# Issuing the gates' last tile in portions between the experts' fetches, in both product-key expert layers

## What is computed

```
act = gelu(einsum('pkd,pd->pk', expert_u[ib], tb)) * gate
out = einsum('pk,pkd->pd', act, expert_v[ib])
```

## Time and profile before

| | |
|---|---|
| median of 3 runs | 4310.23 us (4307.28 to 4312.26) |
| the profiled execution: its own time, its span | 4309.91 us, 4308.1 us |
| PE busy | 3590.4 us, 83% of the span |
| DVE, ACT busy | 2167.2 us (50%), 1557.5 us (36%) |
| wide layer: last tile's store issued, experts' loop ends | 1130 us, about 2065 us |
| narrow layer: the same | 2509.7 us, about 3010 us |
| mean granted clock of TensorE | 0.908 |

### The profile page before, as it was taken

The page is one execution under the profiler, slowest core; times in us unless marked ns, Lnnn a source line. Parts: engine busy times, 40 slices in busy tenths (PEclk is TensorE's granted clock), DMA queues, the critical chain, the costliest instruction groups (busy, mean ns, idle before and its releaser), DMA issues. The chain is left out here.

```text
span 4308.1 us, 55843 instructions
## 1 busy us (share of the span) xinstructions
PE 3590.4 (83%) x19731; PEld 2623.5 (61%) x19731; DVE 2167.2 (50%) x4184; ACT 1557.5 (36%) x2599; POOL 182.2 (4%) x358
## 2 busy tenths in 40 slices
PE   7967978968799999999798479999887867777766
PEld 5747966437688888888567469999656322222222
DVE  4534643799766666666445978888442000000001
ACT  4433442218644434444241466666221111101111
POOL 0006610000000000000000000000100000000000
PEclk8888989989999999999899789999878888888888
DMA  5220021523645545555402089997304799999997
GB/s 189 104 93 13 14 102 45 191 87 157 252 165 193 170 170 195 166 175 195 145 1 88 30 331 335 312 311 240 132 31 174 325 428 427 428 428 428 427 428 320
DMA packets 300729, 909.70 MB, mean 211 GB/s; under 512 B 46736, under 2 KB 150928, under 8 KB 273552
## 3 DMA queue, kind: packets, MB, share of 16 engines
q1 hardware_dynamic: 300560, 907.42, 55.7%
HBM read 854.38 MB, written 52.95 MB: 211 GB/s over the span
## 5 line engine op out<-in xcount | busy, mean ns | idle before, releaser
L1995 PE MATMUL po<-act_parts,v_parts 128*128 128x512 f32 x2048 | 482.0, 393 | 10.7 <-DVE v_parts L2075 4.2
L1982 PE MATMUL pd<-h_parts,u_parts 128*128 128x512 f32 x2048 | 474.2, 392 | 17.5 <-DVE u_parts L2070 17.5
L1982 PEld LDWEIGHTS pd<-h_parts,u_parts 128*128 128x128 f32 x2048 | 387.3, 189 | 99.3 <-DVE u_parts L2070 18.2
L1995 PEld LDWEIGHTS po<-act_parts,v_parts 128*128 128x128 f32 x2048 | 382.7, 188 | 105.1 <-DVE v_parts L2075 22.5
L3543 PE MATMUL pb<-moe_ring_more,moe_xs 128*32 128x512 f32 x2048 | 326.3, 740 | 127.5 <-DMA moe_ring_more<-in_moe_gu 125.9
L3625 DVE TENSOR_TENSOR moe_hidden<-moe_silu,pg 128x512 f32<-128x512 f32 x16 | 11.0, 688 | 575.1 <-PE pg L3532 533.1
L2214 PEld LDWEIGHTS pd<-h_parts,u_parts 128*128 128x128 f32 x2048 | 264.8, 192 | 18.4 <-DVE u_parts L2295 7.4
L2224 PE MATMUL po<-v_parts,act_parts 128*128 128x512 f32 x1024 | 261.5, 400 | 16.6 <-DVE act_parts L2311 16.6
L2214 PE MATMUL pd<-h_parts,u_parts 128*128 128x256 f32 x2048 | 267.9, 284 | 6.8 <-DVE u_parts L2295 6.8
L3568 PE MATMUL pd<-moe_ring_more,moe_hidden 128*32 128x512 f32 x1024 | 167.8, 791 | 107.5 <-DMA moe_ring_more<-in_moe_down 99.3
L395 PE MATMUL ps<-h_terms,w_terms 128*128 128x512 f32 x960 | 225.9, 399 | 36.2 <-DVE w_terms L408 36.2
(11 more groups left out here) (505 smaller groups left out, 5789.1 us busy)
## 6 DMA issues: line engine op xcount, KB each, us to landing
moe_ring_more<-in_moe_gu SPq DMA_DIRECT2D x128, 2048.0 KB, 36.1
u_stream<-in_peer_u SPq DMA_DIRECT2D x256, 512.0 KB, 6.3
v_stream<-in_peer_v SPq DMA_DIRECT2D x256, 512.0 KB, 4.9
moe_ring_more<-in_moe_down SPq DMA_DIRECT2D x64, 2048.0 KB, 36.9
ada_ring<-in_ada_w SPq DMA_DIRECT2D x20, 2048.0 KB, 14.0
g_stream<-peer_gates SPq DMA_DIRECT2D x128, 256.0 KB, 6.1
w_stream<-in_gdn_w_in SPq DMA_DIRECT2D x8, 2048.0 KB, 8.1
w_stream<-in_peer_wq SPq DMA_DIRECT2D x8, 2048.0 KB, 9.2
```

The lines of the kernel that those rows point to most:

```text
L1982: m = pe.matmul(pd[:, j, 0:T], us[:, j, w, c], h[:, w, c], start=(c + w == 0), stop=(c == DC - 1 and w == 1))
L1995: m = pe.matmul(po[:, (c + b) % 4, 0:T], vs[:, j, w, (c + b) * P:(c + b) * P + P], aparts[:, 4 * half + j, w], start=(j + w == 0), stop=(j ...
```

## The change

Four edits in the listing. First, `LastTile` keeps `gates` and the stage, and `write` takes the portions to issue. The scatter now issues portions 0 and 1 in the wide layer, only portion 0 in the narrow one. Second, the wide layer's SP issues portions 2 and 3 after u of period 1. Third, in the wide layer ACT and DVE do all four `high_u(1)` and `low_u(1)` ahead of the first `gate`; ACT does squash 0 and 1 between them and squash 2 and 3 after its wait for portions 1 to 3. Fourth, the narrow layer's SP issues portion 1 after two pairs of gates and v, portion 2 after four pairs, and portion 3 after u 4 to 7, right ahead of the wait for it. No arithmetic is added or taken away, and no byte.

```diff
@@ peer_scatter, SP
-                last.write(sp, gates, stage[(tiles - 1) % 2])
+                last.write(sp, *((0, 1) if T == TALL else (0,)))
@@ LastTile
-    def __init__(self, k, tiles):
+    def __init__(self, k, tiles, gates, stage):
         self.tile = tiles - 1
+        self.gates, self.stage = gates, stage
...
-    def write(self, eng, gates, stage):
-        for n in range(self.PARTS):
+    def write(self, eng, *parts):
+        for n in parts:
             rows = slice(n * self.ROWS, (n + 1) * self.ROWS)
-            eng.dma_start(gates[self.tile, :, rows], stage[:, rows]).then_inc(self.landed[n].h, DMA_DONE)
+            eng.dma_start(self.gates[self.tile, :, rows], self.stage[:, rows]).then_inc(self.landed[n].h, DMA_DONE)
@@ experts_wide, SP
                 for j in range(4):
                     get_u(1, j, False)
+                last.write(sp, 2, 3)
                 last.wait(sp, 0)
                 for j in range(4):
                     get_g(0, j, True)
@@ experts_wide, ACT
                 for j in range(4):
-                    squash(0, j, True)
+                    if j < 2:
+                        squash(0, j, True)
                     high_u(1, j)
-                    if j == 0:
-                        last.wait(sc, 1, 2, 3)
+                last.wait(sc, 1, 2, 3)
+                for j in range(4):
+                    if j >= 2:
+                        squash(0, j, True)
                     high_a(0, 0, j, True)
@@ experts_wide, DVE
                 for j in range(4):
+                    low_u(1, j)
+                for j in range(4):
                     gate(0, j)
-                    low_u(1, j)
                     low_a(0, 0, j)
@@ experts_narrow, SP
                 for j in range(HALF):
                     get_g(0, j)
                     get_v(0, j)
+                    if j == 1:
+                        last.write(sp, 1)
+                last.write(sp, 2)
                 for j in range(HALF, RAW):
                     get_g(0, j)
                 last.wait(sp, 1, 2)
                 for j in range(HALF, RAW):
                     get_u(0, j)
+                last.write(sp, 3)
                 last.wait(sp, 3)
                 for j in range(HALF, RAW):
                     get_v(0, j)
```

More of the change, by code:

```diff
@@ L2371, in peer_layer @@
         gain = k.sb(ctx, "peer_gain", [DC, 2])
-        last = LastTile(k, T // P)
         tables = k.sb(ctx, "u_stream", [4, DC, P])
@@ L2376, in peer_layer @@
             odd = k.sb(place, "gate_stage_odd", [P, P])
+        last = LastTile(k, T // P, gates, (even, odd)[(T // P - 1) % 2])
         u, v = W[f"peer_u{layer}"], W[f"peer_v{layer}"]
```

## The result

The changed kernel takes 4317.92 us (median of 18 runs, 4309.09 to 4327.42) against 4311.57 us before (18 runs, 4307.28 to 4316.85). The ratio is 1.0016, with a 95% interval of 1.0009 to 1.0022: some 7 us slower. I had said 4309.8 with a range to 4315.5; 1.3 us of the distance is that the kernel before itself now stands at 4311.57, where its first three runs had given 4310.23. The loss is smaller than the 0.2% that I had named as the limit, but with the runs made it is clear of the noise, and it went the way that I gave to a rival.

What follows compares the result with a forecast made beforehand. PE alone bounds both loops, so the change acts only at the two starts. From 4309.91, wide -2.3 and narrow +2.0 gave 4309.6 profiled, 4309.9 on the median; stated 4309.8, range 4301 to 4315.5.

Steps and rivals of the forecast that it cites:

- The path: Both starts: first(1) at 1155.3, job 2 waits 3.7 us; narrow second(0) 11.7 us earlier, second(4) held by v 4.
- the narrow layer's queue times: Narrow start: from 2521.6, gates and v pairs 3.4 us, portions 4.9, u 4 to 7 1.25 each; v 4 lands 2556.0.
- The second(4) that I put 2.0 us late: Narrow start: waiting for v 4, second(4) starts at 2558.9 instead of 2556.91; 2.0 us lost, bounds 0 and 6.
- rival B: Narrow start: queue-full stalls delay portion 2 or 3, v 4 lands at 2561.7, 7.7 us lost, total 4315.3; chance 0.17.
- the clock at first(4): Narrow start: first(4) comes 1.3 us earlier, but at half clock after ten idle us, which eats that gain.
- The wide term: Wide start: `low_v` 3 ends at 1180.9 instead of 1183.2, 2.3 us gained; range kept 0.7 to 2.3.
- no loss: Wide start: new waits, shorter than 8.80 us, cost nothing in clock; if it falls, 1.64 of the 2.3 us is lost.
- Rival C: Wide start does nothing, u no earlier or clock falls: 0 to 0.7 gained, 2.0 lost, 4311.5; chance 0.15.
- The price of one DMA: Narrow start: v table into an empty queue 3.5 us by the trace, 3.2 by the skill's fit (loss then 1.6).

Runs made afterwards that it cites:

- n1: Narrow layer's edits alone (wide layer as before), with portion 3 issued together with portion 2, ahead of gates 4 to 7; run once, 4323.08 us.
- t1: Wide layer as before; narrow scatter issues portions 0 to 2, only portion 3 goes out behind u 4 to 7; run once, 4315.14 us.
- t4: Narrow layer's edits alone, plus 96 added matmuls ahead of first(4), overwritten; run once, 4319.85 us.
- e2: The narrow-only kernel: the change's narrow edits, wide layer as before; 4318.97 us, ratio 1.0016 (1.0007 to 1.0025) against before.
- e1: The wide-only kernel: the change's wide edits, narrow layer as before; 4311.64 us, ratio 0.9998 (0.9989 to 1.0007) against before.
- e3: Wide layer's portions moved as in the change, but ACT and DVE in the order of before; narrow layer as before; run once, 4316.38 us.
- ww: Wide edits plus v 0 and v 1 fetched and split ahead of the gates, narrow layer as before; 4311.52 us, ratio 0.9997 (0.9988 to 1.0006).
- e4: Wide layer's edits alone, plus 16, 5 and 8 added matmuls in PE's three waits, overwritten; 4312.78 us, ratio 0.9998 (0.9989 to 1.0007).

## Why the prediction was wrong

**The path was right, in both layers.** The gates land at the same distance as before (35.55 from the first fetch, before 35.53); first(1) starts at 28.6 without a wait (forecast 1155.3 less 1126.66, also 28.6); job 2 waits 3.79 us for squash 2 (3.7); the splits of v 2 and v 3 hold second(0). In the narrow layer second(0) moves 11.6 us forward (11.7), first(4) waits for u 4, and second(4) waits for v 4, which stands behind portion 3. The two halves and n1, t1 and t4 moved these landings, and the starts followed.

**The step that failed is the narrow layer's queue times**, "all from 2521.6" at the full-queue spacing. In the narrow-only kernel, from the first fetch (forecast in brackets, the forecast's times less 2506.37): portion 2 landed at 35.6 (33.5), u 4 at 39.0 (37.2), portion 3 at 49.4 (46.0), v 4 at 52.9 (49.6). I counted 1.25 us for each table of 512 KB, which is what a long queue gives; each time that the queue had run dry while SP waited for a portion (a dry spell), the first tables behind it took more. These are e2's DMA issues, in order v 1 (issued at 2528.70), portion 2 (2534.13), u 4 (2548.67), u 7 (2550.00), portion 3 (2550.48) and v 4 (2562.44), us to landing last:

```profile
v_stream<-in_peer_v SPq DMA_DIRECT2D x1, 512.0 KB, 6.8
...
peer_gates<-gate_stage_odd SPq DMA_DIRECT2D x1, 2048.0 KB, 14.5
...
u_stream<-in_peer_u SPq DMA_DIRECT2D x1, 512.0 KB, 3.4
...
u_stream<-in_peer_u SPq DMA_DIRECT2D x1, 512.0 KB, 7.6
...
peer_gates<-gate_stage_odd SPq DMA_DIRECT2D x1, 2048.0 KB, 12.0
...
v_stream<-in_peer_v SPq DMA_DIRECT2D x1, 512.0 KB, 3.6
```

V 1, the last of the four fetches behind the first dry spell, landed at 22.4 from the first fetch, 2.1 us later than the forecast's sum has it (20.3; 0.2 of it because portion 0 landed later). From there to portion 2 it took 13.1 us, as counted (4.9 + 3.4 + 4.9); the forecast's own sum of this stretch, 2538.4, should read 2538.2. From u 4 to u 7 it took 5.5 us where 3.8 were forecast (5.2 in the changed kernel, whose rows stand above). The two dry spells make up the 3.3 us by which v 4 came late; every other step was within 0.3 us of its forecast. The second(4) that I put 2.0 us late came 5.3 us late (55.8 against 50.5). The landing of v 4 falls beyond the 2556.3 that rival B named (2559.3 on before's scale), though by slow restarts and not by a stalled issue (no issue of e2's narrow start took longer than 1.7 us), and B had 0.17. So B's total of 4315.3 is nearer than mine for another reason than its own.

**A second term I left out:** the clock behind the last narrow wait. In e2 second(4) and the first(7) behind it take 2.65 and 3.09 us instead of 2.03 and 2.08, and the granted clock over 2570:2574 is 0.57 (columns as in the earlier trace rows):

```profile
2570.00:2574.00 4.00, 4.00 (x19) 3.67 (x19) 2.83 (x5) 2.69 (x4) 0.00 (x0) 0.57 1.03 399
```

The 5.3 us at second(4) have become 6.8 us at the end of the layer (521.3 against 514.5). It is the same in the changed kernel (6.2 and 7.8) and in t4 (6.8 and 8.3). In n1 and t1 the clock is up at second(4), and the difference from before stays as it is (8.4 and 8.4, -0.7 and -0.6). I had priced the clock at first(4), where the wait for v 4 covers it, and not behind second(4), where nothing does.

**The wide term was mis-sized too:** 2.3 us forecast, 0.2 in e1, minus 1.4 in the changed kernel's profile. The split of v 3 ended 0.5 to 1.0 us later than forecast, since v 3 took 4.3 to 4.5 us to land instead of 3.5, and the falling clock took 1.7 to 2.8 us where I had taken none and kept 1.64 as the bound. The waits ahead of the slow matmuls were 1.50 and 2.02 us in the changed kernel and 2.57 and 1.08 in e1, each far shorter than the 8.80 removed; behind the 3.79 us wait of job 2 the clock had fallen too (0.66 over 1170:1174), behind e1's of 3.37 us it had not (1.00 over 1164:1168). The Trainium skill ("TensorE: Matmul & The Clock Gate", Why this matters for your kernels) warns against idle gaps between bursts of matmuls. The traces agree with the warning, which was the better guide than my "no loss", and show the fall behind shorter waits than the one it was weighed for. Rival C, which gave the wide part 0 to 0.7 us, had this term right.

**The price of one DMA.** U 4 and v 4, each the first table into a dry queue, landed 3.3 to 3.8 us after their issue in the changed kernel, e2, t4 and (v 4 alone) t1; this term, forecast at 3.6 to 3.7, held. The 3.2 us that the prediction works out from the Trainium skill ("DMA: Bandwidth & Descriptors", Anatomy of one DMA) come from a fit to DMAs that GpSimd issues; SP issues these, and all of them took a little longer.

Sum: -0.2 (wide, e1) and +6.8 (narrow, e2) give +6.6 us against the 6.9 of the ratio; the forecast had -2.3 and +2.0. That the two agree within 0.3 us is partly luck, as each term is read from one trace. What makes the loads behind a restart slow, and why a portion between loads took 6.3 or 6.4 us in three traces (portion 2 in the changed kernel and n1, portion 3 in t4) and 4.9 in e2, stays open.

## What to carry to other kernels

A long queue of DMAs is itself a resource: splitting a store and waiting for its parts in the issuing engine lets the queue run dry, and a dry spell cost some 2 us of latency here (3.3 to 3.8 us until the first table is in, where a long queue brings the next after 1.25 to 1.3) and, behind the first two in e2 and the changed kernel, another 1.4 to 2.0 us of slow loads. That is more than the order won. Before a visible wait is removed, follow the same engine to the next thing that it was just in time for (first(4), 0.36 us) and ask whether that moves as well. A part can be taken out of the front of a queue where it is not needed (portion 3 between u 5 and u 6 gained 2.8 us at second(4)), as long as enough stands behind it to cover the issuer's wait.

## What the runs showed of the hardware that I had not expected

- Of four 512 KB loads issued to a dry queue the third and fourth landed 1.9 and 2.0 us after the one before for u 4 to 7 of the changed kernel (2558.7, 2560.7, 2562.7), in a long queue 1.25 to 1.3. From the first to the fourth it took 4.9 to 5.5 us for u 4 to 7 (the changed kernel, e2, t4) and 4.1 to 5.0 for v 4 to 7 (the same and t1), where a long queue takes 3.8; which of the steps is the long one differs. In the two kernels with portion 3 between u 5 and u 6, where u 6 and u 7 still stood ahead of v 4, the four took 3.8 and 4.0.
- The clock fell in the changed kernel though PE's waits were 1.50 and 2.02 us: with PE 1.27 of 4 us busy it was 0.86, in the next 4 us 0.50.
- An unchanged stage varies between kernels by more than a single profile suggests: the narrow layer, with the same code, took 514.5, 514.8, 516.4, 514.6 and 512.0 us (before, e1, e3, ww, e4) from its first fetch to the copy of the sums. In e3 all of the difference stands at second(4) already (52.4 against 50.5): portion 1 took 5.7 us there instead of 4.9, and the gates landed later behind it. In e4, whose profiled execution is the lowest of its 11 (4303.68 us, median 4312.78), the step is 3.75 us instead of 3.79. For either I have no cause further back, and on this layer's length I took no verdict from less than 2 us in one trace.
